# Gate and up in blocks 1 to 6: four units of seven products, and three low parts summed by DMA

## What is computed

```python
u = rmsnorm(h, pre_ffn_g[i])
ff = (jax.nn.silu(u @ w_gate[i]) * (u @ w_up[i])) @ w_down[i]
h = h + rmsnorm(ff, post_ffn_g[i])
```

## Time and profile before

| | us |
|---|---|
| median of 3 runs | 1075.76 |
| lowest, highest | 1075.71, 1076.46 |
| the profiled execution | 1075.67 |
| its span | 1073.7 |
| PE busy | 1063.8 (99%) |
| DVE busy | 891.5 (83%) |
| ACT busy | 598.3 (56%) |

### The profile page before, as it was taken

The page is one execution under the profiler, slowest core; times in us unless marked ns, Lnnn a source line. Parts: engine busy times, 40 slices in busy tenths (PEclk is TensorE's granted clock), DMA queues, the critical chain, the costliest instruction groups (busy, mean ns, idle before and its releaser), DMA issues. The chain is left out here.

```text
span 1073.7 us, 15358 instructions
## 1 busy us (share of the span) xinstructions
PE 1063.8 (99%) x5731; PEld 921.6 (86%) x5731; DVE 891.5 (83%) x1082; ACT 598.3 (56%) x735; POOL 31.5 (3%) x49
## 2 busy tenths in 40 slices
PE   9999999999999999999999999999999999999997
PEld 8999999999888888888888888888888888888885
DVE  6699987646646787898998998988989899988887
ACT  6554454736545565555565655655655555655553
POOL 6000001101000000000000000000000000000000
PEclk9999999999999999999999999999999999999999
DMA  8655535444386475756756656657656666566665
GB/s 271 216 176 166 172 105 162 135 143 135 112 309 214 140 266 185 225 188 193 223 174 195 216 180 212 195 181 231 189 185 222 223 200 197 189 208 214 208 200 196
DMA packets 113208, 208.06 MB, mean 194 GB/s; under 512 B 9184, under 2 KB 46496, under 8 KB 111856
## 3 DMA queue, kind: packets, MB, share of 16 engines
q1 hardware_dynamic: 111952, 201.49, 58.8%
q10 hardware_dynamic: 608, 4.20, 1.0%
q0 software_dynamic: 576, 1.40, 0.4%
...
## 5 line engine op out<-in xcount | busy, mean ns | idle before, releaser
L561 ACT ACTIVATE w_hi<-raw 128x1024 fp32r<-128x1024 f32 x321 | 337.1, 1059 | 259.0 <-PE ps L1708 153.0
L910 DVE TENSOR_TENSOR w_lo<-raw,w_hi 128x1024 fp32r<-128x1024 f32 x321 | 389.6, 1226 | 84.0 <-ACT w_hi L561 83.4
L1706 PE MATMUL ps<-w_hi,uf 128*128 128x512 f32 x524 | 205.3, 392 | 0.1
L1708 PE MATMUL ps<-w_hi,uf 128*128 128x512 f32 x524 | 204.1, 389 | 0.0
L1707 PE MATMUL ps<-w_lo,uf 128*128 128x512 f32 x524 | 203.9, 389 | 0.0
L1377 PE MATMUL ps<-u,w_hi 128*128 128x272 f32 (+1 forms) x544 | 158.8, 292 | 0.0
L1379 PE MATMUL ps<-u,w_hi 128*128 128x272 f32 (+1 forms) x544 | 155.9, 287 | 0.0
L1380 PE MATMUL ps<-u,w_lo 128*128 128x272 f32 (+1 forms) x544 | 155.7, 286 | 0.0
L841 ACT CAST t_hi<-tx 128x1024 fp32r<-128x1024 f32 x92 | 96.4, 1053 | 67.7 <-DVE tx L1202 56.4
L1708 PEld LDWEIGHTS ps<-w_hi,uf 128*128 128x128 f32 x524 | 98.4, 188 | 20.6
L1706 PEld LDWEIGHTS ps<-w_hi,uf 128*128 128x128 f32 x524 | 98.4, 188 | 20.5 <-issue 0.5
...
## 6 DMA issues: line engine op xcount, KB each, us to landing
raw<-in_w_gate SPq DMA_DIRECT2D x176, 256.0 KB, 3.0
raw<-in_w_up SPq DMA_DIRECT2D x176, 256.0 KB, 3.5
...
arena<-in_x SPq DMA_DIRECT2D x2, 1024.0 KB, 6.2
arena<-in_x ACTq DMA_DIRECT2D x2, 1024.0 KB, 8.7
out<-h2rows SPq DMA_DIRECT2D x2, 1024.0 KB, 5.5
```

Of the source, the lines that this page charges most:

```text
L561: act.activation(w_hi[:, slot, :], raw[:, slot, :], ACT.Copy).then_inc(hi_done, 1)
L910: dve.tensor_tensor(w_lo[:, slot, :], raw[:, slot, :], hi_view(w_hi[:, slot, :]), ALU.subtract).then_inc(lo_done, 1)
L1706: pe.matmul(o, a[0], b[0], start=start, stop=False)
L1708: return pe.matmul(o, a[1], b[0], start=False, stop=stop)
```

## The change

1. In blocks 1 to 6 the table reads `PPZZPZZP` instead of `PPZPZPZP`: four units rather than three, in two pairs (chunks 4 to 7 and 10 to 13). Blocks 7 to 10 keep the old table. The left sums of a fourth pair are made in block 0.
2. The units of these blocks alternate between `tx`, `t_hi`, `t_lo` and a second set `tx2`, `t_hi2`, `t_lo2`. These, `gated` and three buffers `lo_extra` lie in the part of `ffn` that later blocks fill.
3. In the same blocks DVE does not make the low parts of the plain chunks 1, 2 and 8 (`ADDED_CH`). ACT writes the negative of such a chunk, rounded, into `lo_extra` (`minus_hi`, one chunk ahead, before its own split), POOL issues a DMA that adds `raw` to it, and SP waits for that DMA before it loads over the raw slot. PE does for such a chunk first the eight matmuls with `w_hi`, then the four with `lo_extra`.

```diff
-    SEVEN_F, SEVEN_U = (0, 1, 2), (11, 12, 13, 14, 15, 16, 17, 18, 19)
+    SEVEN_F, SEVEN_U = (0, 1, 2, 3), (11, 12, 13, 14, 15, 16, 17, 18, 19)
     SUM_AT = {4: 11, 10: 12, 12: 13, 18: 14, 22: 15, 24: 16, 28: 17, 32: 18, 36: 19}
     SUM_NO = {d: i for i, d in enumerate(SUM_AT.values())}
-    F_SUM_AT = {10: 0, 12: 1, 14: 2}
-    ROUND = ["PPPPPPPP"] + ["PPZPZPZP"] * (NFG - 1) + ["PPPPZPPZPPZPPZPZPZPZPP", "PPPZPZPZPZPZPZPZPZPZPP"]
+    F_SUM_AT = {10: 0, 12: 1, 13: 2, 14: 3}
+    WITH_SPARE = range(1, 7)
+    ADDED_CH = (1, 2, 8)
+    ROUND = ["PPPPPPPP"] + ["PPZZPZZP" if g in WITH_SPARE else "PPZPZPZP" for g in range(1, NFG)] + ["PPPPZPPZPPZPPZPZPZPZPP", "PPPZPZPZPZPZPZPZPZPZPP"]
...
+    ADDED = [BEGIN[g] + ch for g in WITH_SPARE for ch in ADDED_CH]
+    ADDED_NO = {q: i for i, q in enumerate(ADDED)}
+
+    def lo_by_dve(q):
+
+        return q + 1 - sum(1 for a in ADDED if a <= q)
+
+    def lo_by_dma(q):
+
+        return ADDED_NO[q] % len(ADDED_CH), 16 * (ADDED_NO[q] // len(ADDED_CH) + 1)
...
+    def buffers_of(z):
+
+        g, d = SEVENS[z]
+        return (z - SEVENS_TO[g - 1]) % 2 if g in WITH_SPARE else 0
+
+    def before_in_buffers(z):
+
+        return max((y for y in range(z) if buffers_of(y) == buffers_of(z)), default=None)
...
+        a_spare = top[0] + 4 * KT * SEQ + 4 * 1152 + 4 * 4 * (max(WITH_SPARE) + 1) * 2 * SEQ
+        tx2 = sb_at("tx2", [P, 4, DCOLS], F32, a_spare)
+        t_lo2 = sb_at("t_lo2", [P, 4, DCOLS], F32R, a_spare)
+        t_hi2 = sb_at("t_hi2", [P, 4, DCOLS], F32R, a_spare + 16 * DCOLS)
+        lo_extra = [sb_at(f"lo_extra{i}", [P, CE], F32R, a_spare + at)[:, :] for i, at in enumerate((32 * DCOLS, 40 * DCOLS, 56 * DCOLS))]
+        sums_of, hi_of, lo_of = (tx, tx2), (t_hi, t_hi2), (t_lo, t_lo2)
...
-        gated = sb_at("gated", [P, NQ, DCOLS], F32, a_y + 4 * KT * SEQ - 8 * DCOLS)
+        gated = sb_at("gated", [P, NQ, DCOLS], F32, a_spare + 48 * DCOLS)
...
-                sp_eng.wait_ge(lo_done, q - WSLOTS + 1)
+                if q - WSLOTS in ADDED_NO:
+                    i, n = lo_by_dma(q - WSLOTS)
+                    sp_eng.wait_ge(hi_done, q - WSLOTS + 1)
+                    sp_eng.wait_ge(lo_added[i], n)
+                else:
+                    sp_eng.wait_ge(lo_done, lo_by_dve(q - WSLOTS))
...
+            for q in ADDED:
+                i, n = lo_by_dma(q)
+                pool.wait_ge(neg_done, ADDED_NO[q] + 1)
+                pool.dma_start(lo_extra[i].bitcast(F32), raw[:, q % WSLOTS, :], accum_op=ALU.add).then_inc(lo_added[i], 16)
...
+            def minus_hi(q):
+                slot = q % WSLOTS
+                act.wait_ge(raw_landed[slot], landed(q))
+                if ADDED_NO[q] >= len(ADDED_CH):
+                    act.wait_ge(chunks_used, ADDED[ADDED_NO[q] - len(ADDED_CH)] + 1)
+                act.activation(lo_extra[lo_by_dma(q)[0]], raw[:, slot, :], ACT.Copy, scale=-1.0).then_inc(neg_done, 1)
...
                     z = SEVEN_NO.get((g, d))
+                    if q + 1 in ADDED_NO:
+                        minus_hi(q + 1)
                     if z is not None and ch % 2 == 0:
                         first_half_hi(q)
...
+                sums, y = sums_of[buffers_of(z)], before_in_buffers(z)
                 if z == 0:
                     dve.wait_ge(s_lo, 2 * len(SEVEN_F))
-                else:
-                    dve.wait_ge(t_used, 4 * z - 3)
+                if y is not None:
+                    dve.wait_ge(t_used, 4 * y + 1)
+                if y is not None and buffers_of(z) == 0:
                     dve.wait_ge(fold_done, len(QUARTERS) * max(min(SEVENS[z][0], NFG) - 1, 0))
-                dve.tensor_tensor(tx[:, 0, :], b12, b11, ALU.add).then_inc(t_made, 1)
+                dve.tensor_tensor(sums[:, 0, :], b12, b11, ALU.add).then_inc(t_made, 1)
...
-                    if z is None:
+                    if z is None and q not in ADDED_NO:
                         split(q)
...
+                if q in ADDED_NO:
+                    pe.wait_ge(hi_done, q + 1)
+                    for m, j in quarters:
+                        for h in range(2):
+                            pe.matmul(quarter(g, m, j), left(g, kt, m)[h], right(q, j)[0], start=ch == 0 and h == 0, stop=False)
+                    i, n = lo_by_dma(q)
+                    pe.wait_ge(lo_added[i], n)
+                    for m, j in quarters:
+                        mm = pe.matmul(quarter(g, m, j), left(g, kt, m)[0], lo_extra[i][:, j * DCOLS:(j + 1) * DCOLS],
+                                       start=False, stop=ch == chs - 1)
+                    return mm
+                pe.wait_ge(lo_done, lo_by_dve(q))
```

More of the change, by code:

```diff
@@ L199, in build_trunk @@
         sums_f = sb_at("sums_f", [P, len(SEVEN_F), 4, 2, P], F32R, a_y)
-        gated = sb_at("gated", [P, NQ, DCOLS], F32, a_y + 4 * KT * SEQ - 8 * DCOLS)
+        gated = sb_at("gated", [P, NQ, DCOLS], F32, a_spare + 48 * DCOLS)
         sums_y = sb_at("sums_y", [P, max(len(SEVEN_U) - IN_U, 1), 3, 2, P], F32R, a_y)
-        assert 32 * P * len(SEVEN_F) + 8 * DCOLS <= 4 * KT * SEQ and 24 * P * (len(SEVEN_U) - IN_U) <= 4 * KT * SEQ
+        assert 32 * P * len(SEVEN_F) <= 4 * KT * SEQ and 24 * P * (len(SEVEN_U) - IN_U) <= 4 * KT * SEQ
         side = sb_at("side", [P, KT * SEQ], F32, a_y)
@@ L207, in build_trunk @@
         a_ff = place(4 * FT * 2 * SEQ)
+        assert a_spare == a_ff + 4 * 28 * 2 * SEQ
         ffn = sb_at("ffn", [P, FT, 2, SEQ], F32R, a_ff)
@@ L348, in build_trunk @@
             sem(n) for n in ("rows_done", "turned", "h2_hi", "h2_lo", "h2_sq", "r2c_done"))
+        neg_done, lo_added = sem("neg_done"), [sem(f"lo_added{i}") for i in range(len(ADDED_CH))]
         silu_done, p_done, f_hi, f_lo = (sem(n) for n in ("silu_done", "p_done", "f_hi", "f_lo"))
@@ L838, in weight_sums_hi @@
             def weight_sums_hi(z):
+                b = buffers_of(z)
                 for h in range(2):
                     act.wait_ge(t_made, 3 * z + h + 2)
-                    act.copy(t_hi[:, 2 * h:2 * h + 2, :], tx[:, 2 * h:2 * h + 2, :]).then_inc(t_hi_done, 1)
+                    act.copy(hi_of[b][:, 2 * h:2 * h + 2, :], sums_of[b][:, 2 * h:2 * h + 2, :]).then_inc(t_hi_done, 1)
             def row_sums_hi(d):
@@ L1191, in weight_sums @@
                     dve.wait_ge(raw_landed[at[k]], landed(q - 1 + k))
+                sums, y = sums_of[buffers_of(z)], before_in_buffers(z)
                 if z == 0:
                     dve.wait_ge(s_lo, 2 * len(SEVEN_F))
-                else:
-                    dve.wait_ge(t_used, 4 * z - 3)
+                if y is not None:
+                    dve.wait_ge(t_used, 4 * y + 1)
+                if y is not None and buffers_of(z) == 0:
                     dve.wait_ge(fold_done, len(QUARTERS) * max(min(SEVENS[z][0], NFG) - 1, 0))
-                dve.tensor_tensor(tx[:, 0, :], b12, b11, ALU.add).then_inc(t_made, 1)
+                dve.tensor_tensor(sums[:, 0, :], b12, b11, ALU.add).then_inc(t_made, 1)
                 first_half_lo(q - 1)
-                if z:
-                    dve.wait_ge(t_used, 4 * z - 2)
+                if y is not None:
+                    dve.wait_ge(t_used, 4 * y + 2)
                 dve.wait_ge(t_made, 3 * z + 1)
-                dve.tensor_tensor(tx[:, 1, :], b22, tx[:, 0, :], ALU.subtract).then_inc(t_made, 1)
-                if z:
-                    dve.wait_ge(t_used, 4 * z)
+                dve.tensor_tensor(sums[:, 1, :], b22, sums[:, 0, :], ALU.subtract).then_inc(t_made, 1)
+                if y is not None:
+                    dve.wait_ge(t_used, 4 * y + 4)
                 dve.wait_ge(t_made, 3 * z + 2)
-                dve.tensor_tensor(tx[:, 2:4, :], raw[:, at[0]:at[0] + 2, 0:DCOLS],
-                                  tx[:, 1:2, :].to_broadcast([P, 2, DCOLS]), ALU.add).then_inc(t_made, 1)
+                dve.tensor_tensor(sums[:, 2:4, :], raw[:, at[0]:at[0] + 2, 0:DCOLS],
+                                  sums[:, 1:2, :].to_broadcast([P, 2, DCOLS]), ALU.add).then_inc(t_made, 1)
             def weight_sums_lo(z):
+                b = buffers_of(z)
                 dve.wait_ge(t_made, 3 * z + 3)
@@ L1303, in _ @@
                         inner_product(g - 1)
-                    if z is None:
+                    if z is None and q not in ADDED_NO:
                         split(q)
-                    elif ch % 2:
+                    elif z is not None and ch % 2:
                         weight_sums(q, z)
@@ L1740, in weight_sum @@
                 def weight_sum(t):
-                    return [t_hi[:, t, :], t_lo[:, t, :]]
-                pe.wait_ge(lo_done, q + 1)
+                    return [hi_of[buffers_of(z)][:, t, :], lo_of[buffers_of(z)][:, t, :]]
+                pe.wait_ge(lo_done, lo_by_dve(q))
                 if g < NFG:
```

7 lines of the change are left out of this document (3 added, 4 removed).

## The result

The changed kernel takes 1099.45 us (1098.51 to 1100.49, five runs), the one before, beside it, 1075.76. The ratio is 1.0219, 95% interval 1.0207 to 1.0230: slower by 23.7 us. The forecast was 1089.4, range 1078 to 1112, slower with 0.86. The side was right and so was the kind of mechanism; the size was 10 us short.

A forecast was written before the change was run, and what follows sets the result against it. PE's matmul count bounded the kernel; after the change, a chain through DVE, ACT and loads. From 1075.67 us, block 1 +0.4 and blocks 2 to 6 +13.3 (-4.1 matmuls, +17.8 waits) gave 1089.4 us, range 1078 to 1112.

The forecast's parts named there:

- 18 matmuls fewer, 4.1 us: PE, blocks 1 to 6: one more unit each, 21 matmuls for 24, six times: -4.1 us.
- DVE has no slack at the second unit: Paired units: DVE's first unit may begin at most 5.19 us after PE's block end; each later us costs PE one.
- The fold chain: Blocks 2 to 6: loads of chunks 11 and 2, negative, split, bank copy, fold, next first unit: 45.05 us per block.
- the wait for chunk 11: DVE's third unit, otherwise starting 15.34 us after the first, waits for chunk 11's load until 16.7 us.
- Where PE waits: PE in blocks 2 to 6: waits of 3.3 us per block, at chunk 2's transposes and in the second and fourth unit.
- The transfer's time: Accumulating DMA of 512 KB, issue to landing, called A: taken as 7.5 us, range 4.9 to 12.
- The limit of 7.65: Accumulating transfer's time in us above which every further us costs one us per block.
- the slot chain: Sum of chunk 1 must land before chunk 5 loads and the first unit starts: 44.9 us with a 7.5 us transfer.
- Its traffic at nothing: The 18 transfers of 512 KB cost nothing in traffic, the DMA engines having 0.37 of the time free.
- One value for every load: Weight loads in the block chain: 4.2 us to landing for chunk 11, 3.0 us for chunk 2, in every block.
- The clock in full: PE in the gate and up blocks: clock granted 1.00, the 2.4 GHz level, matmuls 0.2268 us each.
- The rival on the slow side: Accumulating transfer bounds every block: at A = 10 us, 2.35 us more per block, 1103.5 us; chance of over 1100 0.18.

The follow-up runs named there:

- the pair of runs with early and late negative: Changed kernel with only chunks 2 and 8 summed by DMA; negative of chunk 2 before, or after, chunk 1's split and the bank copy: 1098.89 and 1085.07 us.
- The idle sums: Changed kernel with only chunk 8 summed by DMA, plus two 512 KB accumulating transfers per block into free buffers, their results unused: 1090.42 us.

## Why the prediction was right, and where it was short

- *18 matmuls fewer, 4.1 us.* Right, by the sum of intervals above.
- *DVE has no slack at the second unit.* Right: with no transfer at all the fourth unit already costs 9.3 us, and taking one low part from before the first unit gives 4.9 us back.
- *The fold chain.* Right in kind and in its order, and shown by the pair of runs with early and late negative. The three terms from the folds to the first unit, and the wait for chunk 11, came as written. The blocks were 46.5 us on average and not 45.05, and at two of the five turns the other chain, over chunk 5, was the longer by 0.6 and 0.7 us.
- *Where PE waits.* Wrong in place: the wait is at the block's first matmul, on the fold's sums, which the text did not see in PE's program. Of 17.2 us of waits 3.2 are in the units, as named. For the sum it made little difference as far as can be argued, since a block takes the length of the chain wherever PE stands still.
- *The transfer's time.* Taken as 7.5; the sums of chunk 1 took 4.8 to 6.2 us, of chunk 2 7.3 to 8.2, of chunk 8 4.5 to 5.0. The median 5.9 lies under the estimate. The limit of 7.65 was not passed by chunk 1, and yet the slot chain was as long as the fold chain: in blocks 2 to 6 the sum of chunk 1 was 1.3 to 2.7 us shorter than the 7.5, and the load of chunk 5 behind it took 5.4 to 6.0 us with its issue rather than 3.4. The two errors nearly cancel; that this chain came out near its 44.9 is luck. The lone transfer took 4.5 us. The estimate of 4.4 us from the Trainium skill, DMA: Bandwidth & Descriptors, "Anatomy of one DMA", with the bytes doubled after the half rate of Collectives: The Full Stack, "The bandwidth ceiling" (a rule that the page gives for its collective rings), agrees with it; for two sums at once, 7.3 to 8.2 us, it was too low.
- *Its traffic at nothing.* **This term failed.** It was put at nothing because the DMA engines have 0.37 of the time free, which is an average; in the 8 us of the row above they have none free. Beside the sums of chunks 1 and 2 the up half of chunk 4 took 7.2 to 8.0 us to land in blocks 1 to 6, where it took 3.5 to 4.7 in the same blocks of the kernel before. The issue of the changed kernel between 548.1 and 549.0 us:

```profile
raw<-in_w_up SPq DMA_DIRECT2D x1, 256.0 KB, 8.0
```

and the up half of chunk 5, between 552.5 and 553.3:

```profile
raw<-in_w_up SPq DMA_DIRECT2D x1, 256.0 KB, 5.1
```

Against them stand 3.0 to 4.8 in the earlier trace rows. What it cost directly is the time by which first units waited for chunk 5: 1.4 us in block 1 and 0.6 and 0.7 us in two later blocks, 2.7 of the missing 10.0. The idle sums put 3.4 to 4.6 us on the traffic of two transfers per block.
- *One value for every load.* **This failed too.** The chain took 4.2 us for chunk 11 and 3.0 for chunk 2. In the changed kernel chunk 11 took 4.2 to 6.0, issued just as the sum of chunk 8 landed, and chunk 1 of block 6 took 6.5 with no sum on the way. The kernel without any sum has such a load too (6.2 us), and missed its own forecast by 4 us. These long loads hold 4.4 of the missing 10.0 us; their cause stays open (with no chunk summed chunk 11 took 4.1 to 4.6, so a part of it may be traffic after all).
- *The clock in full.* That it could fall behind a wait was not considered: 7.0 us of matmuls at the lower clock. It is not simply added to the blocks, since DVE's chain runs on meanwhile; but in the block shown ACT's split of chunk 5 waited for PE to use up chunk 1 and DVE behind it 0.71 us (the row at 562.00), which is on the chain; in this block and the next the load of chunk 11 went out 0.8 and 0.6 us late.
- *The sum.* Five distances between first units, 1.45 us longer each, are 7.3 of the missing 10.0 us. Of these 4.0 stand before the third unit (it began 16.5 to 18.5 us after the first, not 16.7; 2.6 of them the loads of chunk 11, 1.4 ACT's split behind the slow PE), 1.8 at the load of chunk 1 of block 6, 1.3 are the two waits for chunk 5. Block 1, whose first unit waited 1.39 us for chunk 5, gives 1.4; the rest lies at the turn into block 7.

The rival on the slow side, the transfer as bound with 1103.5 at A = 10, came within some 4 us in its number, and not for its reason: no sum in the change took the 10 us, and the slot chain it names set only some of the blocks.
